# Neighbourhood attention by column strips: 8 grid columns by 16 rows a query block, tokens stored column by column

## The reference

```
grid: 16 rows x 64 columns of tokens, token = 64 * row + column;  256 more context tokens
6 heads of 64;  WIN_H = 8, WIN_W = 16
rows of a query at row r:      first = clip(r - 4, 0, 8),   8 rows
columns of a query at column c: first = clip(c - 8, 0, 48), 16 columns
s_loc = q . k (in the window) * scale + rpb[head, key row - r + 7, key column - c + 15]
s_ctx = q . k (256 context tokens) * scale
p = softmax(concat(s_loc, s_ctx));  y = (p @ v) * silu(g)
hybrid layer 0 also attends from the 256 context tokens to the context; layer 1 does not
```

## Time and profile before

| | |
|---|---|
| median of three runs | 3222.98 us (3219.58 to 3223.21) |
| the profiled execution | 3222.22 us, its span 3220.4 us |
| mean granted TensorE clock | 0.997 of full |
| busy: PE, DVE, ACT, POOL | 98%, 44%, 39%, 25% of the span |
| DMA queue q1 (SP), q10 (ACT) | 14.7% and 13.2% of 16 DMA engines |
| neighbourhood attention | about 2090 to 2342 us (layer 0) and 2825 to 3130 us (layer 1, with the end of its projections) |
| `pad_rows` on SP | 803.98 us and 864.31 us |

### The profile page before, as it was taken

How to read it: one execution, slowest core, us unless ns; L and a number is a source line. 1 busy time by engine, 2 the same in 40 slices (tenths; PEclk the granted TensorE clock), 3 DMA queues, 4 the chain that set the end, 5 groups by cost and what they waited for, 6 DMA issues and landing times.

```text
span 3220.4 us, 48521 instructions
## 1 busy us (share of the span) xinstructions
PE 3156.3 (98%) x19411; PEld 2561.4 (80%) x19411; DVE 1433.0 (44%) x3305; ACT 1255.0 (39%) x2582; POOL 805.0 (25%) x407
## 2 busy tenths in 40 slices
PE   7999999999999998999999999999999999999999
PEld 6877778787887876777888888877788788877787
DVE  3342122221213125569333446554546845564566
ACT  4444444443443334412322433255343433354342
POOL 2155455111111124223154111100223111111231
PEclk9999999999999999999999999999999999999999
DMA  6113323143523233323354311111003332111113
GB/s 194 45 48 86 80 64 85 52 127 117 154 90 90 93 94 105 118 73 105 139 182 151 97 42 44 44 34 32 27 21 117 105 81 49 45 39 32 33 41 143
DMA packets 314342, 267.26 MB, mean 83 GB/s; under 512 B 63365, under 2 KB 276697, under 8 KB 314122
## 3 DMA queue, kind: packets, MB, share of 16 engines
q1 hardware_dynamic: 198970, 133.71, 14.7%
q10 hardware_dynamic: 115152, 130.49, 13.2%
HBM read 220.87 MB, written 48.58 MB: 84 GB/s over the span
## 4 chain that ended last, share of the span: by engine, by line
PE 52%; DVE 4%; ACT 2%; issue 2%; DMA 1%; ACTq 0%; POOL 0%; DVEq 0%; SPq 0%; POOLq 0%
PE psum L1493 25%; PE psum L383 8%; PE psum L308 5%; PE psum L1627 2%; PE psum L1607 2%; PE psum L1616 2%; PE psum L3097 1%; PE psum L1530 1%; DVE act_lo L2520 1%; PE psum L1520 1%; PE psum L3088 1%; PE psum L3072 0%; PE psum L1536 0%; PE psum L1563 0%; DVE arena L2282 0%
## 5 line engine op out<-in xcount | busy, mean ns | idle before, releaser
L2700 POOL TENSOR_TENSOR w_lo<-w_raw,w_hi 128x1024 fp32r<-128x1024 f32 x122 | 296.4, 2429 | 1481.2 <-ACT w_hi L3178 768.3
L1493 PE MATMUL psum<-act_hi,w_hi 128*128 128x512 f32 (+1 forms) x1376 | 513.0, 373 | 5.1 <-DVE act_lo L456 3.3
L2870 PE MATMUL psum<-act_hi,w_hi 128*128 128x512 f32 x1280 | 505.6, 395 | 4.8 <-ACT arena L1191 3.9
L2870 PE MATMUL psum<-act_lo,w_hi 128*128 128x512 f32 x1280 | 507.7, 397 | 0.0
L1493 PE MATMUL psum<-act_lo,w_hi 128*128 128x512 f32 (+1 forms) x1376 | 504.4, 367 | 0.0
L2870 PE MATMUL psum<-act_hi,w_lo 128*128 128x512 f32 x1280 | 504.2, 394 | 0.0
L1493 PE MATMUL psum<-act_hi,w_lo 128*128 128x512 f32 (+1 forms) x1376 | 504.1, 366 | 0.0
L3651 DVE CUSTOM_DVE_ANT_0 arena<-psum,arena 128x128 f32<-128x128 f32 (+1 forms) x384 | 112.1, 348 | 479.9 <-PE psum L2909 332.7
L1493 PEld LDWEIGHTS psum<-act_hi,w_hi 128*128 128x128 f32 x1376 | 260.6, 189 | 58.0 <-issue 15.0
L1493 PEld LDWEIGHTS psum<-act_hi,w_lo 128*128 128x128 f32 x1376 | 260.4, 189 | 44.8 <-issue 5.0
L1493 PEld LDWEIGHTS psum<-act_lo,w_hi 128*128 128x128 f32 x1376 | 260.9, 190 | 42.3 <-issue 5.5
(11 more groups left out here) (402 smaller groups left out, 5391.4 us busy)
## 6 DMA issues: line engine op xcount, KB each, us to landing
w_raw<-in_attn_w_in SPq DMA_DIRECT2D x80, 512.0 KB, 3.8
w_raw<-in_w_in SPq DMA_DIRECT2D x64, 512.0 KB, 4.0
spare<-in_w_mod ACTq DMA_DIRECT2D x24, 1024.0 KB, 7.8
x<-arena ACTq DMA_DIRECT2D x24, 512.0 KB, 2.9
arena<-weight_rows ACTq DMA_DIRECT2D x16, 512.0 KB, 6.7
w_raw<-in_ssm_w_in SPq DMA_DIRECT2D x16, 512.0 KB, 3.7
arena<-mc_mat ACTq DMA_DIRECT2D x16, 512.0 KB, 3.6
arena<-x ACTq DMA_DIRECT2D x16, 512.0 KB, 5.5
```

Source lines behind the costliest of these rows:

```text
L1493: ins = nc.tensor.matmul(psum[:, n % 2, 0:c], w[:, slot % 2, k * P:(k + 1) * P], a[:, k, c0:c0 + c], start=(m == 0), stop=(m == 23))
L2700: G.tensor_tensor(w_lo[:, par], w_raw[:, par], w_hi[:, par].bitcast(F32), ALU.subtract).then_inc(slot_split, 1)
L2870: ins = nc.tensor.matmul(psum[:, h % 2, :], w[:, (3 + j) % 2, k * P:(k + 1) * P], a[:, k, c:c + 512], start=(m == 0), stop=(m == 23))
```

## The change

Grid tokens of the neighbourhood groups (queries, keys, values, not the gate) are now stored column by column, 16 rows of a column together: `evac` writes them in that order. A query block is 8 columns by 16 rows. Its keys are its own strip of 8 columns and its neighbours, 3 strips (384 keys) for blocks 1 to 6 and 2 (256 keys) for blocks 0 and 7. The mask now holds the row window and the column window, and one bias table serves all blocks but the two at the edges, which get another (`mask_edges`). `evacuate` writes back to row order. The padded bias is turned over (31 columns by 15 rows), the skewed table is 16 x 31 x 16 instead of 64 x 15 x 64, and `load_bias` fetches it in 8 pieces of 16 partitions a head instead of 2 of 64.

```diff
-        N_LOG = 896
-        BT = [[region(25600, 14, 64), region(26496, 14, 64)], [region(21376, 14, 64), region(0, 14, 64)]]
+        N_LOC = 384
+        N_LOG = N_LOC + CTX
+        BT = [[region(25616, 2, N_LOC), region(26384, 2, N_LOC)], [region(21376, 2, N_LOC), region(0, 2, N_LOC)]]
-        ORDER2 = (0, 1, 6, 7, 2, 3, 4, 5, 8, 9)
+        ORDER2 = (1, 2, 3, 4, 5, 6, 0, 7, 8, 9)
...
+            first = max(b - 1, 0)
+            return first, min(b + 2, GRID_BLOCKS) - first
...
-            return [(first // 2 + i, i) for i in range((count + 1) // 2)] + [(8, 5), (9, 6)]
+            return [(first + i, i) for i in range(count)] + [(8, 3), (9, 4)]
...
-                sp.dma_start(PAD[0:15, h, 48:79], io["na_rpb_2"][l, h]).then_inc(n_bias, 16)
+                sp.dma_start(PAD[0:31, h, 8:23], io["na_rpb_2"][l, h].rearrange("a k -> k a"),
+                             allow_slow_non_contiguous=True).then_inc(n_bias, 16)
-            sp.dma_start(rpb_pad[l].rearrange("h a k -> a h k"), PAD[0:15]).then_inc(n_padded, 16)
+            sp.dma_start(rpb_pad[l].rearrange("h k a -> k h a"), PAD[0:31]).then_inc(n_padded, 16)
-                sp.dma_start(rpb_skew[l, h].rearrange("q a c -> a q c"),
-                             bass.AP(tensor=src.tensor, offset=src.offset + 63, ap=[[P, 15], [-1, 64], [1, 64]])
+                sp.dma_start(rpb_skew[l, h].rearrange("r k a -> k r a"),
+                             bass.AP(tensor=src.tensor, offset=src.offset + 15, ap=[[31, 31], [-1, 16], [1, 16]])
...
-                    for half in range(2):
-                        act.dma_start(BT[hp % 2][h][HALF[half]], src[:, 1 - half:15 - half, :]).then_inc(n_bt[hp % 2], 16)
+                    for c in range(8):
+                        act.dma_start(BT[hp % 2][h][16 * c:16 * c + 16, 1, :],
+                                      rpb_skew[l, 2 * hp + h, :, 7 - c:31 - c, :].rearrange("r k a -> r (k a)")
+                                      ).then_inc(n_bt[hp % 2], 16)
...
+                if q < 3:
+                    dst = (tk, tq, tv)[q][:, c0:c0 + c]
+                    if j >= 3 and c0 < S:
+                        dst = strips((tk, tq, tv)[q])[:, c0 // 64:(c0 + c) // 64, :]
+                        src = src.rearrange("p (r c) -> p r c", c=64)
...
-                def mask_middle():
+                def mask_edges():
...
-                fresh = {0: [logs[b][h] for b in range(2) for h in range(2)], 1: [], 2: [logs[1][1]]}[hp]
-                for log in fresh:
-                    own(V.memset(log[:, 512:640], 0.0))
```

More of the change, by code:

```diff
@@ L103, in window_mask @@
 def window_mask():
[L105 to L108, removed]
+    r = np.arange(16)
+    first = np.clip(r - 4, 0, 8)
+    rows = (r[None] >= first[:, None]) & (r[None] < first[:, None] + 8)
+    d = np.arange(24)[None] - 8 - np.arange(8)[:, None]
+    cols = (d >= -8) & (d < 8)
+    both = cols[:, None, :, None] & rows[None, :, None, :]
+    inside = np.concatenate([both.reshape(P, 384), np.tile(rows, (8, 1))], 1)
+    return np.where(inside, np.float32(0), np.float32(NEG)).astype(np.float32)
 def constants():
@@ L1407, in window_of, with bias_of, strips, grid_block @@
                 return 0, 0
-            return row_start(2 * b), row_start(2 * b + 1) + 8 - row_start(2 * b)
+            first = max(b - 1, 0)
+            return first, min(b + 2, GRID_BLOCKS) - first
         def tiles_of(n):
             first, count = window_of(n)
-            return [(first // 2 + i, i) for i in range((count + 1) // 2)] + [(8, 5), (9, 6)]
+            return [(first + i, i) for i in range(count)] + [(8, 3), (9, 4)]
+        def bias_of(bt, n):
+            first, count = window_of(n)
+            if count == 3:
+                return bt[:, 0]
+            at = P if first == 0 else 0
+            return bt[:, 1, at:at + P * count]
+        def strips(v):
+            return v[:, 0:S].rearrange("p (c r) -> p r c", r=16)
+        def grid_block(v, b):
+            return v[:, 0:S].rearrange("p (r c) -> p c r", c=64)[:, 8 * b:8 * b + 8, :]
         def queries(n):
@@ L1599, in scores @@
                     first, count = window_of(n)
-                    pieces = [(3, 64, S, CTX)]
-                    if count > 8:
-                        pieces = [(3, 0, 64 * first + 512, 64)] + pieces
+                    pieces = [(3, S, CTX)]
                     if count > 0:
-                        pieces = [(2, 0, 64 * first, 512)] + pieces
-                    for bank, to, c0, c in pieces:
+                        pieces = [(2, P * first, P * count)] + pieces
+                    for bank, c0, c in pieces:
                         for h in range(2):
-                            ins = nc.tensor.matmul(psum[:, bank + 2 * h, to:to + c], tq[HALF[h], queries(n)],
+                            ins = nc.tensor.matmul(psum[:, bank + 2 * h, 0:c], tq[HALF[h], queries(n)],
                                                    tk[HALF[h], c0:c0 + c], start=True, stop=True)
@@ L1714, in evac @@
                         act.wait_ge(u_evac, block_base(l, 1))
[L1715 to L1722, removed]
+                if q < 3:
[3 more added lines that the diff above has]
+                        src = src.rearrange("p (r c) -> p r c", c=64)
+                    C.activation(dst, src, ACT.Copy, scale=SCALE if (j < 3 and q == 0) or (j >= 3 and q == 1) else 1.0
+                                 ).then_inc(g_evac[n % 2], 1)
                 if q == 3:
@@ L1809, in probs @@
                                      accum_out=st[:, 0:1]).then_inc(u_probs, 1)
-                    C.activation(log[:, 640:N_LOG], psum[:, 3 + 2 * h, 64:64 + CTX], ACT.Exp, bias=st[:, 4:5],
+                    C.activation(log[:, N_LOC:N_LOG], psum[:, 3 + 2 * h, 0:CTX], ACT.Exp, bias=st[:, 4:5],
                                  accum_out=st[:, 1:2]).then_inc(u_probs, 1)
@@ L2042, in logits @@
                     if count > 0:
-                        at = first - 2 * ORDER2[n] + 6
-                        V.tensor_tensor_reduce(log[:, 0:64 * count], flat(2 + 2 * h, 2)[:, 0:64 * count],
-                                               bt[h][:, at:at + count, :].rearrange("p a c -> p (a c)"),
+                        V.tensor_tensor_reduce(log[:, 0:P * count], psum[:, 2 + 2 * h, 0:P * count], bias_of(bt[h], n),
                                                1.0, -3e38, ALU.add, ALU.max, accum_out=st[:, 2:3]).then_inc(u_logits, 1)
-                    V.tensor_reduce(st[:, 3:4], psum[:, 3 + 2 * h, 64:64 + CTX], AX.X, ALU.max).then_inc(u_logits, 1)
+                    V.tensor_reduce(st[:, 3:4], psum[:, 3 + 2 * h, 0:CTX], AX.X, ALU.max).then_inc(u_logits, 1)
                     dve.wait_ge(u_logits, h0 + halves_before(m + 1))
@@ L2067, in evacuate @@
                     dve.wait_ge(u_scores, b0 + min(n + 3, NB[l]))
-                    V.tensor_tensor(Y2[:, hp + 5, queries(n)], psum[:, 3, 384:512], ng[:, queries(n)], ALU.mult).then_inc(u_evac, 1)
+                    y, o, g_ = Y2[:, hp + 5, queries(n)], psum[:, 3, 384:512], ng[:, queries(n)]
+                    if n < GRID_BLOCKS:
+                        b = ORDER2[n]
+                        y, o, g_ = grid_block(Y2[:, hp + 5], b), o.rearrange("p (c r) -> p c r", r=16), grid_block(ng, b)
+                    V.tensor_tensor(y, o, g_, ALU.mult).then_inc(u_evac, 1)
                 def conv_steps(x0, x1):
@@ L2074, in conv_steps @@
                             conv_step(*conv[x])
-                def mask_middle():
+                def mask_edges():
+                    rows = NMASK[:, N_LOC:].rearrange("p (o r) -> p o r", o=1).to_broadcast([P, 24, 16])
                     for h in range(2):
-                        own(V.memset(bt[h][HALF[0], 10, :], NEG))
-                        own(V.memset(bt[h][HALF[1], 2, :], NEG))
+                        raw = bt[h][:, 1].rearrange("p (c r) -> p c r", r=16)
+                        own(V.tensor_tensor(raw, raw, rows, ALU.add))
                 dve.wait_ge(v_turned, VT_DONE + 6 * l + 2 * hp + 1)
                 V.tensor_copy(VR2[:, 0:8].rearrange("p a c -> p (a c)"), flat(2, 2)).then_inc(v_rows[1], 1)
-                fresh = {0: [logs[b][h] for b in range(2) for h in range(2)], 1: [], 2: [logs[1][1]]}[hp]
-                for log in fresh:
-                    own(V.memset(log[:, 512:640], 0.0))
                 dve.wait_ge(n_mask, 16 * (l + 1))
-                dve.wait_ge(n_bt[hp % 2], 16 * 4 * ((l + 1) if hp == 1 else 2 * l + hp // 2 + 1))
+                dve.wait_ge(n_bt[hp % 2], 16 * 16 * ((l + 1) if hp == 1 else 2 * l + hp // 2 + 1))
                 for h in range(2):
-                    own(V.tensor_tensor(bt[h], bt[h], NMASK.rearrange("p (o c) -> p o c", o=1).to_broadcast([P, 14, 64]), ALU.add))
+                    own(V.tensor_tensor(bt[h][:, 0], bt[h][:, 1], NMASK[:, 0:N_LOC], ALU.add))
                 if hp == 2:
@@ L2103, in nat_segment @@
                         evacuate(n - 1)
-                    if n + 1 == EDGES:
```

(3 more changed lines are left out.)

32 lines of the change are left out of this document (14 added, 18 removed).

## The result

The changed kernel takes 3244.97 us (median of four runs, 3241.28 to 3248.35) where the kernel before takes 3221.28 us beside it on the same chip (3217.68 to 3223.21): ratio 1.0076, 95% interval 1.0062 to 1.0090. It is 24 us slower; 31 were forecast. The profiled execution after is the lowest of the four, 3241.28 us, with a span of 3239.1 us, 18.7 us longer than the span before.

What follows compares the result with a forecast made beforehand. PE was taken to bound the neighbourhood segments, with SP's DMA queue priced separately in the first attention layer: -53.8 + 17.4 + 64 + 3.4 = +31 us on 3222.2, so 3253 us, range 3195 to 3300.

Steps and rivals of the forecast that it cites:

- The attention's saving: Neighbourhood segments: fewer transposes, products with V and score columns save PE 53.8 us, give or take 3.
- `load_bias`: Neighbourhood segments: sixteen issues hold ACT 8.0 us, PE waits 5.4 and 3.3 us per layer, 17.4 us over two layers.
- Two stalls, 3.4 us in all: First attention layer: after each of the two `pad_rows` pauses PE runs at a lower clock, 3.4 us together.
- One engine for 31 rows: `pad_rows`: 31 has no divisor but 1 up to 16, so each DMA of 31 outer rows runs on one engine.
- `pad_rows`, 64 us: First attention layer: one-engine DMAs delay the weight load behind them, stalling 33 and 31 us; ends 40 and 115.
- The play of 5 us: First attention layer: ACT's idle time plus PE's later need let the weight load come 5 us late without stalling PE.
- the 4-byte packet: Six bias loads in `pad_rows`: 8.8 ns a packet on one engine, adding 24.6 us to the present 7.8.
- the 64-byte copy: Six DRAM to DRAM copies in `pad_rows`: 2982 packets at 12 ns, between 10.7 and 20.6, taking 35.8 us.
- one engine's 6%: Trace sign for `pad_rows`: the queue shows one DMA engine's share, 6%, during PE's pauses of about 30 us.
- B: `pad_rows`: loads land before ACT rounds them, under 43 us from `pad_rows` to landing; 3186 us, or 3176; chance 0.18.
- C: `pad_rows`: the full ring also holds back ACT's DMAs, two or three more 10 us stalls; 3275 to 3300 us; chance 0.12.
- D: Neighbourhood segments: ACT becomes the bound through 36 slow evacuations, at worst 15 us more than summed; chance 0.03.

Runs made afterwards that it cites:

- both cures: The changed kernel with every 31-row DMA cut into 16 and 15 rows and whole bias tables fetched with 2 issues: 3174.46 us, ratio 0.9845 to the kernel before.
- two issues: The changed kernel with each head's whole bias table laid out in DRAM ahead and fetched by one DMA, 2 issues instead of 16: 3223.07 us, ratio 1.0001.
- split all: The changed kernel with each 31-row DMA in `pad_rows` (loads, store, copies) cut into 16 and 15 rows: 3197.58 us, ratio 0.9911 to the kernel before.
- the old kernel with sixteen issues: The kernel before with only its four bias loads of 64 partitions cut into sixteen of 16 partitions: 3247.35 us, ratio 1.0072.
- the plain evacuations: The changed kernel with 31-row DMAs cut and 2 bias issues, but `evac` writing in row order, so its output differs: 3172.58 us.

## Why the prediction was right, and what it mis-sized

**The attention's saving** of 53.8 us measured 53.6 in the changed kernel; at the full clock, in the kernel with both cures, it is 231.5 - 176.5 = 55.0.

**`load_bias`.** 17.4 us of waits were forecast and 17.0 are what two issues take away; 5.4 and 3.3 in the first layer measured 5.30 and 3.13, and 8.0 us of issue 7.55. One detail was wrong: PE waited not for `take_pt` but for the evacuation ahead of it, whose bank the projection needed. **The step that failed is the clock's: "Two stalls, 3.4 us in all" counted the low clock behind the two long stalls alone.** It also follows the waits of 5.3 and 3.1 us, and cost 9.4 us there (8.0 in the projection, 1.4 in the attention; 6.6 in "split all", where one wait of 3.1 us left the clock full) and 7.6 in the old kernel with sixteen issues. The earlier trace rows had shown it after a wait of over 4 us; the term should have been applied to the prediction's own 5.4.

**One engine for 31 rows.** Right, to the packet. The Trainium skill (DMA: Bandwidth & Descriptors, the section on why a DMA increments its semaphore by 16) gives the largest divisor up to 16; the trace agrees with 3836, 187 and 4016 packets. The Trainium skill (DMA: Bandwidth & Descriptors, Queues, rings and completion order) says that each engine takes its descriptors in the order of the ring, and the trace agrees: the copies close one after another, and the weight load behind them lands late. Queue q1 in 835 to 868, and the row of the weight loads from the profile's page (KB each, median us to landing):

```profile
q1 hardware_dynamic: 2361, 0.15, 8.9%
...
w_raw<-in_attn_w_in SPq DMA_DIRECT2D x80, 512.0 KB, 3.8
```

Of the copies' 2982 packets some 600 were left when the weight load was issued at 868.49; at 11.8 ns they are 7 us, and the load was rounded at 877.60, 9.1 us after its issue, where such a load lands after 3.8.

**`pad_rows`, 64 us and 3.4 for the clock behind it,** was 42.7 in all, of which 41.0 are PE's two pauses (33 and 31 forecast, 24.0 and 17.0 measured). The landing was put at 885.3 (885 when rounded) and the rounding of the weights began at 877.6. Of the 7.7 us between, 5.7 are the loads (32.4 forecast, 26.7 measured), 0.9 the store, 0.6 the start, 0.6 the copies and the landing (43.8 forecast; 834.37 to 877.60 is 43.2). In the second call, from its first load to the rounding, 73.7 were forecast and 62.7 passed: the loads took 20.7, the store 4.2, the rest 37.9 for 36.8. The play of 5 us held in the first call, where ACT idled 28.9 and PE 24.0; in the second it was 8.1 (25.1 and 17.0), so 3 us of the miss are there.

So the mis-sized term is above all the 4-byte packet. 8.8 ns came from the queue's share of busy time, and the measured share gives as much, 0.087 x 16 x 14 us / 2160 = 9.0 ns; but by the time elapsed a packet passed every 14 us / 2160 = 6.5 ns, below the 7 of the prediction's own lower end. And the 64-byte copy was right by luck. By the share it is 0.109 x 16 x 22 / 1858 = 20.7 ns, the upper bound of the prediction and not the 12 chosen "since size sets most of it"; by the time elapsed it is 22 / 1858 = 11.8. The share adds up the times of packets that overlap on their engine, so it bounds the pace from above and does not give it. That is also why the queue shows 8.7% and 10.9% where the prediction expected one engine's 6%.

**The rivals.** B fell with the packet counts and the two pauses; at 74 and 63 us per call it was far from its 43. C did not show: PE has two pauses there and no third of such size. D fell with the plain evacuations.

**How 31 became 19.** `pad_rows` with its clock 24.7 too high, `load_bias` 0.4, the saving 1.2 too low; the clock behind the short waits 9.4, other short waits 3.4, which the text took as hidden (L1644 waits for exponentials six times, 3.4 us, where L1627 before waited 2.0), and 1.2 of projection, all missing: 31.0 - 24.7 - 0.4 - 1.2 + 9.4 + 3.4 + 1.2 = 18.7 us of span. Errors of both signs cancelled in part, so that the total came out near is in part luck. That the medians differ by 23.7 and the spans by 18.7 is mostly because the profiled execution was the fastest of its four, 3.7 us under their median.

## What to carry to other kernels

When a tensor's outer dimension changes, look up every DMA that has it as outermost dimension: 15 rows to 31 turned a 7.8 us stage into 26.7, and cutting 31 into 16 + 15 brought it to 11.8 and PE's pauses to nothing. Count the DMA issues that stand in a row ahead of an evacuation, and price a wait on the tensor engine with the matmuls that follow it at the low clock, which added 9 us to 17 here. And when a change saves work in one place and loses more, look for the hole in the slices before giving the idea up: with both repairs the strips are 1.5% faster than before.

## What the runs showed of the hardware

- Packets of one DMA on one engine overlap in the records: the queue's share gave 20.7 ns for a 64-byte DRAM to DRAM packet and 9.0 for a 4-byte one, while one passed every 11.8 and 6.5 ns. In the packet records a 4-byte packet lasts 9 ns and the next starts 6 ns after it.
- An engine that issues DMAs into a backlog is itself held: one copy's issue took 0.6 us at the least and 10.8 at the most (below, in ns, min/median/max). The six loads held SP 22.9 us while ACT's 1 MB loads were under way, 16.7 without them.

```profile
L1470 SPq DMA_DIRECT2D rpb_skew<-rpb_pad x12: 583/5784/10823, 834.4 to 937.5; - x12
```
- A wait of 5.3 us was followed by 4 us at half the clock and 4 at 0.74. The same wait of 3.1 us was followed by 0.56 in one kernel and by the full clock in another.
